# A transformer layer in split single precision: VectorE one operand ahead in the first two pairs, and four other pieces of work at other steps

## The reference, cut to what matters

```python
h    = rms_norm(x, pre_norm)
proj = h @ w_in_a                       # 1024 x (3072 + 1536 + 512)
b, c, u = split(proj[:, :3072])
mix  = b * conv3(c * u)                 # causal, 3 taps, per feature
gate = proj[:, 3072:4608]
mq   = proj[:, 4608:]                   # queries of 4 heads of 128
kv   = rms_norm(mem, mem_norm) @ w_mem_kv          # 256 memory rows
mem_o = softmax(q k^T / sqrt(128)) v               # per head
y    = concat(mix, mem_o) * silu(gate) @ w_out     # 1536 x 1024
x    = x + rms_norm(y, post_norm)
```

## Time and profile before

| | us |
|---|---|
| median of three executions | 2271.42 |
| profiled execution, own time | 2269.35 |
| its span, first to last instruction | 2267.6 |
| TensorE busy | 2188.2 (97%) |
| VectorE busy | 1211.8 (53%) |
| ScalarE busy | 732.4 (32%) |
| mean granted TensorE clock | 0.992 |

### The profile page before, as it was taken

The page is one execution under the profiler, slowest core; times in us unless marked ns, Lnnn a source line. Parts: engine busy times, 40 slices in busy tenths (PEclk is TensorE's granted clock), DMA queues, the critical chain, the costliest instruction groups (busy, mean ns, idle before and its releaser), DMA issues.

```text
span 2267.6 us, 26778 instructions
## 1 busy us (share of the span) xinstructions
PE 2188.2 (97%) x9950; PEld 1811.7 (80%) x9950; DVE 1211.8 (53%) x1885; ACT 732.4 (32%) x1296; POOL 100.8 (4%) x155
## 2 busy tenths in 40 slices
PE   5899999999999999999999999999999899999998
PEld 3687878788888888888887788888888688888886
DVE  7677776713534351355235227575754855555554
ACT  4433433421121131122113333545341533333332
POOL 0000000000000000000000000000000000000000
PEclk9999999999999999999999999999999999999999
DMA  4786667677666577756667565656667433333331
GB/s 172 271 307 249 253 239 263 253 257 250 205 204 214 195 243 268 250 187 206 212 212 275 177 209 192 218 189 210 197 205 289 142 121 130 130 130 127 129 117 65
DMA packets 140880, 462.64 MB, mean 204 GB/s; under 512 B 15664, under 2 KB 15696, under 8 KB 137808
## 3 DMA queue, kind: packets, MB, share of 16 engines
q1 hardware_dynamic: 119952, 385.40, 48.6%
q0 software_dynamic: 20800, 75.53, 10.3%
HBM read 328.75 MB, written 132.12 MB: 203 GB/s over the span
## 4 chain that ended last, share of the span: by engine, by line
PE 85%; DVE 9%; issue 2%; ACT 2%; DMA 1%; SPq 0%; DVEq 0%; ACTq 0%
PE banks L1413 28%; PE banks L1414 28%; PE banks L1415 28%; DVE hop_lo L1015 3%; PE banks L1528 1%; DVE x_in L1011 1%; DVE slots L1044 1%; ACT hop_hi L737 1%; DMA slots<-w_split 1%; DVE x_in L986 1%; ACT probs L811 1%; DVE pt_lo L1179 0%; DVE st_w L1039 0%; PE banks L1434 0%; DMA raws<-in_w_kv 0%
## 5 line engine op out<-in xcount | busy, mean ns | idle before, releaser
L1413 PE MATMUL banks<-hop_hi,slots 128*128 128x512 f32 x2688 | 1058.6, 394 | 32.0 <-DVE p L1096 9.8
L1414 PE MATMUL banks<-hop_lo,slots 128*128 128x512 f32 x2688 | 1050.9, 391 | 0.0
L1415 PE MATMUL banks<-hop_hi,slots 128*128 128x512 f32 x2688 | 1050.4, 391 | 0.0
L1413 PEld LDWEIGHTS banks<-hop_hi,slots 128*128 128x128 f32 x2688 | 507.9, 189 | 145.4 <-issue 20.5
L1415 PEld LDWEIGHTS banks<-hop_hi,slots 128*128 128x128 f32 x2688 | 507.3, 189 | 107.0
L1414 PEld LDWEIGHTS banks<-hop_lo,slots 128*128 128x128 f32 x2688 | 508.3, 189 | 103.8 <-issue 1.4
L1044 DVE TENSOR_TENSOR slots<-raws,slots 128x512 fp32r<-128x512 f32 x154 | 105.2, 690 | 131.6 <-ACT slots L692 131.1
L748 ACT ACTIVATE s<-banks 128x512 f32<-128x512 f32 x95 | 56.9, 598 | 355.3 <-PE banks L1415 355.3
L1096 DVE TENSOR_TENSOR u<-banks,u 128x512 f32<-128x512 f32 x55 | 38.0, 690 | 212.5 <-PE banks L1415 212.5
L692 ACT ACTIVATE slots<-raws 128x512 fp32r<-128x512 f32 x154 | 95.5, 626 | 155.5 <-PE banks L1415 128.4
L692 ACT ACTIVATE slots<-st_w 128x512 fp32r<-128x512 f32 x140 | 87.8, 627 | 169.2 <-PE banks L1415 126.4
(11 more groups left out here) (163 smaller groups left out, 1985.1 us busy)
## 6 DMA issues: line engine op xcount, KB each, us to landing
slots<-w_split SPq DMA_DIRECT2D x420, 512.0 KB, 3.4
w_split<-slots SPq DMA_DIRECT2D x140, 512.0 KB, 3.1
raws<-in_w_in SPq DMA_DIRECT2D x78, 256.0 KB, 3.8
x_in<-in_x_t SPq DMA_DIRECT2D x16, 1024.0 KB, 6.9
g_kept<-mix POOLq DMA_DIRECT2D x32, 512.0 KB, 6.2
raws<-g_kept SPq DMA_DIRECT2D x64, 256.0 KB, 3.9
x_zb<-in_x POOLq DMA_DIRECT2D x22, 512.0 KB, 4.1
out_x<-x_zb POOLq DMA_DIRECT2D x21, 512.0 KB, 4.1
```

The lines of the kernel that those rows point to most:

```text
L1413: nc.tensor.matmul(dst, a, c, start=first, stop=False, skip_group_check=True)
L1414: nc.tensor.matmul(dst, a, d, start=False, stop=False, skip_group_check=True)
L1415: return nc.tensor.matmul(dst, b, c, start=False, stop=last, skip_group_check=True)
```

## The change

Six edits:

1. **First two pairs.** ScalarE and VectorE get an order written out by hand. `token_sum(0, 2)` stands ahead of `operand_lo` of R6; ScalarE makes the operands of R3, R7 and R2 each one product sooner; the adds of R3 and R7 stand behind the splits of R2; the four units of pair 2 stand behind the splits of R4, and the Silu reads of R2 and R4 behind ScalarE's part of these four units.
2. **Next tokens' work.** `prefetch_steps` is (41, 51, 63), (69, 79, 91) instead of (45, 55, 59), (66, 76, 80), and `token_sum(m + 1, 0)` is at step 99 instead of 92.
3. **Memory's loads.** Behind the load of the memory the two blocks of key and value weights follow four and seven steps later, the two queries ten and twelve.
4. **Memory's chain.** Root and inverse at the head of step 12, spread behind step 12 instead of 14, normalising in steps 13 and 14 instead of 15 and 16, `mem_hi` in step 15 and `mem_lo` in 16 instead of both in 17.
5. **Seam to the output.** `operand_hi` of R2 goes from the last step of macro 3 behind the reads of n = 0; R4's from n = 1 to 2; `WM_HI` from n = 2, 3 to 3, 4. On VectorE `operand_lo` of R2 and `token_sum(OUT, 3)` go from n = 0 to 1, `operand_lo` of R4 from 1 to 3, `WM_LO` from 3, 4 to 4, 5.
6. **Probabilities in halves.** `pt_hi` and `pt_lo` are made as two instructions of 512 columns each, one for each bank, and `weigh` waits for each half ahead of its three matmuls.

```diff
-            return (45, 55, 59), (66, 76, 80)
+            return (41, 51, 63), (69, 79, 91)
...
                             sp.dma_start(mem_in[:], mem).then_inc(mem_dma, 16)
-                            load_kv(0)
-                            load_kv(1)
-                            load_q(0)
-                            load_q(1)
+                        if now in (6, 9):
+                            load_kv((now - 6) // 3)
+                        if now in (12, 14):
+                            load_q((now - 12) // 2)
...
-                nc.scalar.activation(flat(pt_hi[:]), flat(probs_t), ACT.Copy).then_inc(pt_hi_done, 1)
+                for a in range(MT):
+                    nc.scalar.activation(pt_hi[:, a, :], probs_t[:, a, :], ACT.Copy).then_inc(pt_hi_done, 1)
...
-                if step == 12:
-                    root(NT, NM)
-                if step == 17:
+                if step == 15:
                     act.wait_ge(normed, NT * KT + KT)
                     nc.scalar.activation(mem_hi[:], mem_in[:], ACT.Copy).then_inc(mem_hi_done, 1)
...
+            def both_hi(r):
+                unit_hi(0, r)
+                unit_hi(1, r)
+
+            def evacuate_both(r):
+                evacuate(0, r)
+                evacuate(1, r)
...
-            unit_hi(0, R5)
-            unit_hi(1, R5)
             operand_hi(0, R5)
-
-
-            for r in range(PRODUCTS):
-                if r in (R1, R5, R6):
-                    evacuate(0, r)
-                    evacuate(1, r)
-                if r + 2 < PRODUCTS:
-                    operand_hi(0, r + 2)
-                ahead(0, 2 * r)
-                ahead(0, 2 * r + 1)
-                if r not in (R1, R5, R6):
-                    evacuate(0, r)
-                    evacuate(1, r)
+            both_hi(R5)
+            evacuate_both(R1)
+            operand_hi(0, R6)
+            operand_hi(0, R3)
+            both_hi(R6)
+            operand_hi(0, R7)
+            evacuate_both(R5)
+            both_hi(R3)
+            operand_hi(0, R2)
+            evacuate_both(R6)
+            both_hi(R7)
+            both_hi(R2)
+            operand_hi(0, R4)
+            evacuate_both(R3)
+            both_hi(R4)
+            evacuate_both(R7)
+            for n in range(4):
+                unit_hi(*ORDER[len(FIRST_TWO) + n])
+            evacuate_both(R2)
+            evacuate_both(R4)
...
+                        if step == 12:
+                            root(NT, NM)
                         attention(step)
...
-                    if i == PAIRS - 1 and r != R6:
+                    if i == PAIRS - 1 and r != R6 and (m + 1 < OUT or r != R4):
                         operand_hi(m + 1, {R1: R1, R5: R5, R3: R6, R7: R3, R2: R7, R4: R2}[r])
...
-                if n == 1:
+                if n == 0:
+                    operand_hi(OUT, R2)
+                if n == 2:
                     operand_hi(OUT, R4)
-                if n == 2:
+                if n == 3:
...
-                if n == 3:
+                if n == 4:
...
-                dve.wait_ge(pt_hi_done, n + 1)
-                nc.vector.tensor_tensor(flat(pt_lo[:]), flat(probs_t), flat(pt_hi[:]).bitcast(f32),
-                                        ALU.subtract).then_inc(pt_lo_done, 1)
+                for a in range(MT):
+                    dve.wait_ge(pt_hi_done, MT * n + a + 1)
+                    nc.vector.tensor_tensor(pt_lo[:, a, :], probs_t[:, a, :], pt_hi[:, a, :].bitcast(f32),
+                                            ALU.subtract).then_inc(pt_lo_done, 1)
...
-                if step == 13:
-                    inverse(NT, NM)
-                if 15 <= step < 17:
+                if 13 <= step < 15:
...
-                if step == 17:
+                if step == 16:
                     dve.wait_ge(mem_hi_done, 1)
...
+            token_sum(0, 1)
+            sum_first_two(R6)
+            token_sum(0, 2)
+            operand_lo(0, R6)
+            split_first(R6)
+            sum_first_two(R3)
+            operand_lo(0, R3)
+            split_first(R3)
+            for k in range(HK, KT):
+                norm(0, k)
+            sum_first_two(R7)
+            operand_lo(0, R7)
+            split_first(R7)
+            operand_lo(0, R2)
+            token_sum(0, 3)
+            split_first(R2)
+            add_first_two(R3)
+            add_first_two(R7)
+            operand_lo(0, R4)
+            split_first(R4)
+            build(*ORDER[len(FIRST_TWO)])
+            build(*ORDER[len(FIRST_TWO) + 1])
+            add_first_two(R2)
+            build(*ORDER[len(FIRST_TWO) + 2])
+            build(*ORDER[len(FIRST_TWO) + 3])
...
-                        if step == 92:
+                        if step == 99:
                             token_sum(m + 1, 0)
...
-                if n == 0:
+                if n == 1:
                     operand_lo(OUT, R2)
                     token_sum(OUT, 3)
-                if n == 1:
+                if n == 3:
                     operand_lo(OUT, R4)
                 ahead(OUT, n)
-                if n in (3, 4):
-                    half = n - 3
+                if n in (4, 5):
+                    half = n - 4
...
-                pe.wait_ge(pt_lo_done, n + 1)
                 for a in range(MT):
+                    pe.wait_ge(pt_lo_done, MT * n + a + 1)
...
-                        if step == 14:
+                        if step == 12:
                             spread(NT, NM)
```

More of the change, by code:

```diff
@@ L1215, in memory @@
                                                 ALU.add).then_inc(acc_done, 1)
-                if step == 13:
-                    inverse(NT, NM)
-                if 15 <= step < 17:
+                if 13 <= step < 15:
                     dve.wait_ge(spread_done, NT + 1)
-                    for k in range(HK * (step - 15), HK * (step - 15) + HK):
+                    for k in range(HK * (step - 13), HK * (step - 13) + HK):
                         row = mem_in[:, k, :]
@@ L1249, in sum_first_two, with add_first_two @@
                 weight_sum(1, r)
+            def add_first_two(r):
+                add(0, r)
+                add(1, r)
             def split_first(r):
@@ L1273, in _ @@
             split_first(R5)
-            for r in range(PRODUCTS):
-                if r + 2 == R6:
-                    token_sum(0, 1)
-                if r + 2 == R7:
-                    token_sum(0, 2)
-                if r + 2 == R2:
-                    for k in range(HK, KT):
-                        norm(0, k)
-                if r + 2 == R4:
-                    token_sum(0, 3)
-                if r + 2 < R2:
-                    sum_first_two(r + 2)
-                if r + 2 < PRODUCTS:
-                    operand_lo(0, r + 2)
-                    split_first(r + 2)
-                else:
-                    ahead(0, 2 * r)
-                    ahead(0, 2 * r + 1)
-                if r in (R3, R7, R2):
-                    add(0, r)
-                    add(1, r)
+            token_sum(0, 1)
[23 more added lines that the diff above has]
+            build(*ORDER[len(FIRST_TWO) + 3])
             for p in range(2, ALL_PAIRS):
@@ L1307, in _ @@
                             keys_values(KV_AT.index(step - 2))
+                        if step == 12:
+                            inverse(NT, NM)
                         attention(step)
```

## The result

| | before | changed |
|---|---|---|
| median, us | 2272.59 (4 runs, 2270.12 to 2274.65) | 2240.79 (4 runs, 2240.09 to 2242.08) |
| profiled execution, own time | 2269.35 | 2240.83 |
| its span | 2267.6 | 2238.7 |
| TensorE busy | 2188.2 | 2181.0 |

The ratio is 0.9867, 95% interval 0.9854 to 0.9881: 31.8 us faster by the medians, 28.9 by the two spans. The forecast was 2239.5, and 31.9 us off the profiled execution's own time, which came out 28.5 shorter.

A forecast was written before the change was run, and what follows sets the result against it. Bound by TensorE's matmuls, busy 97% of the span. Terms 7.2 + 7.9 + 5.2 + 6.8 + 6.8 - 2.0 = 31.9 us off 2269.35 give 2237.4, for a median 2239.5; range 2230 to 2250.

The forecast's parts named there:

- The first two pairs: Start of the kernel: the hand-written order starts pair 2 at 82.6 instead of 89.79, gain 7.2 us, bounds 0 and 10.
- the hand schedule: First two pairs followed: R6 starts at 50.5, R7 at 62.5, R4 at 74.4, pair 2 at 82.6.
- Next tokens' work: Macro 0: waits before the first tile's spread and at the second tile's norms go, gain 7.9 us, bounds 3 and 8.5.
- rival (c): Norms late in their new place in all three macros, slower at 2281 us; chance 0.03, shared with an unseen loss.
- Loads: Last macro, step 7: the weight unit no longer waits behind blocks and queries, gain 5.2 us, bounds 3.5 and 5.4.
- Chain: First key block: wait falls from 4.9 to 1.5 us without low clock, gain 3.4 + 3.4 = 6.8, bounds 3.4 and 8.3.
- Halves: `weigh` in the heads: of eight waits for `pt_lo` two vanish, six lose 0.98 us; gain 6.8, bounds 3 and 8.6.
- Seam: First output pair: R4 3.4 us earlier, all spent before M0, low clock likely; -2.0 us, bounds -4 and +4.
- The sum: All six parts together: 31.9 us off the profiled execution's 2269.35, giving 2237.4, or a median of 2239.5.
- rival (b): Remaining waits: the clock keeps falling, four more low-clock stretches of 1.7 us give 2246; chance 0.27 together with another rival.

The follow-up runs named there:

- f1_reads: Changed kernel with ScalarE reading R2 and pair 0's R4 ahead of pair 2's second and fourth units, VectorE adding R2 ahead of pair 2's units: 2236.38 us.
- u2_tokens: Changed kernel with the next tokens' squares, sums, norms and first token sum put back to their old steps: 2249.93 us, ratio 0.9900 to the kernel before.
- u6_halves: Changed kernel with the probabilities' high and low part made as one instruction each again: 2245.85 us, ratio 0.9883 to the kernel before.
- g1_add: Changed kernel with f1_reads's edit and the memory's second output weights split first, plus R7's add ahead of R4's low operand in the first output pair: 2231.05 us.

## Why the prediction was right, and where it was not

- **The first two pairs**: right in mechanism and size, 7.0 against 7.2, with R6, R7, R4 and pair 2 within 0.2 us of the hand schedule. ScalarE became late before pair 2 as worked out, and in `f1_reads`, with the Silus and the fourth unit in another order (and one add of VectorE sooner), this wait is gone.
- **Next tokens' work**: right, 8.1 against 7.9 by the side-by-side table, and `u2_tokens` takes it away in macro 0 alone. Of the rival (c), norms late in the new place, there is no sign.
- **Loads**: right in mechanism. Two things made loads and chain's wait 6.9 instead of 8.6. The unit of step 11 is issued behind the first block of key and value weights and lands 0.38 us late (0.54 with restart), which I had called "alone between units"; of all the profiles with the new loads only this one shows that wait. And there is a stretch of low clock at 429.42 in the changed kernel's profile that the one before lacks. It is counted in this line of the table: about 1 us, since at the next seam the two kernels stand 14.1 apart instead of 15.1.
- **Chain**: the wait is 1.40 where 1.5 was forecast. The term that was mis-sized is its clock: 2.3 instead of 3.4, because half of a low-clock stretch's length is lost only where TensorE has work, and part of this one covered idle time. The row was there to be read: TensorE is busy for 5.46 of its 6.83 us, and half of that is 2.7.
- **Halves**: right, 6.7 against 6.8, and 6.2 in `u6_halves` over the same steps. (The 0.98 us by which each half was to be sooner is 0.94 by the durations quoted, 1.01 + 1.22 less 0.60 + 0.69.)
- **Seam**: right in mechanism: the gain up to R4 is spent before M0. That the loss is 2.1 against 2.0 is in part luck: 1.7 of it is a stretch of low clock that stands behind M0 in five profiles of eight and costs nothing in the other three. I had found no later place where TensorE waits for something with a time of its own; M0 became one, and it took up to 1.8 us of what was lost just ahead of it.
- **The sum**: 31.9 against 28.8 by the traces. The whole difference is the 1.7 of the loads and the chain's wait, the 1.1 of the chain's clock, and tenths. Some 2.1 of it is low clock, given back less than I priced (1.1) or falling at a new place (1.0), so rival (b) held in a small part; the late unit at step 11 is 0.5 more.

## What to carry to other kernels

Where one engine is busy for 97%, a list of its idle times with who ended each is the budget: each was followed to the next thing that is late. For the first two pairs, the next tokens' work and the halves those sums held to 0.2 us; for the loads and the chain they were off by 0.5 to 1.1 in a DMA's landing and in what the low clock costs, which a list of waits does not hold. Work moved ahead of a wait may only pass the wait on to the next instruction of the same queue, as at M0; look at what the last item of the moved group now stands behind. Splitting an instruction pays, in spite of its fixed cost, where the reader waits for it and can begin with the first part.

## What the runs showed of the hardware

- One program's low-clock stretches fall at different places in different executions, with the same waits: behind pair 2 (at 83.8) in one profile of the changed kernel, at 429.4 in the other. The eight timed executions of this kernel span 2238.81 to 2242.50, so two profiles can differ by some 2 us or more of 2240 with the same waits. Two kernels' profiles are better compared over the stretch that the edit touches than by their spans: `g1_add` looks 1.3 us faster by its span and is 0.1 faster there.
- Low clock costs at most half of the time in which TensorE is busy under it: 2.3 us for a stretch of 6.83 with 5.46 busy. Where TensorE would next have waited for something else it costs nothing: ahead of M0 in three profiles, 1.5 to 3.0 behind it in five.
- ScalarE reading one PSUM bank while VectorE reads the other costs next to nothing: in the changed kernel VectorE's first half, which overlaps ScalarE's second, takes 0.69 us, and its second half, alone, 0.68.
